# Gate-column strip moved behind the delta-rule projections; their first unit's products woven between the turns of x

## The reference, cut to what matters

```python
h = rmsnorm(x, g_mix)
proj = jnp.einsum('btd,de->bte', h, w_in)
gq, gk, gv, gr, glr, cqkv, dz, da, db = jnp.split(proj, _split_points(IN_SIZES), axis=-1)
...
gate_pre = jnp.einsum('btr,rk->btk', glr, gla_w_gate2) + gla_b_gate
...
xc = jnp.concatenate([conv_buf.astype(cqkv.dtype), cqkv], axis=1)
conv = jax.nn.silu(sum(xc[:, j:j + T] * gdn_conv_w[j] for j in range(CONV_W)))
```

## Time and profile before

| | |
|---|---|
| median of 3 runs | 1779.99 us (1779.85 to 1781.88) |
| the profiled execution, its own time | 1779.38 us |
| its span from first to last instruction | 1777.7 us |
| TensorE busy | 1753.1 us, 99% |
| VectorE, ScalarE, GpSimd busy | 1078.1, 761.8, 173.2 us |
| weights and data read | 347.84 MB |

### The profile page before, as it was taken

One profiled execution on the slowest core, in us unless ns is written; L12 is line 12 of the kernel. 1 busy time (PEld: TensorE's weight loads), 2 busy tenths in 40 slices (PEclk: granted clock), 3 DMA queues, 4 the chain that ended last, 5 costly groups with the idle time before them and its releaser, 6 DMA issues.

```text
span 1777.7 us, 35497 instructions
## 1 busy us (share of the span) xinstructions
PE 1753.1 (99%) x14527; PEld 1676.6 (94%) x14527; DVE 1078.1 (61%) x1502; ACT 761.8 (43%) x801; POOL 173.2 (10%) x170
## 2 busy tenths in 40 slices
PE   8999999999999999999999999999999999999997
PEld 6999999988999998886799999999999999999997
DVE  6778447746676776653376666665444666655444
ACT  6554546445733433433323444443333444443444
POOL 4000001001055000000035200000000000000231
PEclk9999999999999999999999999999999999999999
DMA  8555645561566679778846788885557988874553
GB/s 274 163 173 188 189 143 174 164 208 48 176 214 197 207 270 330 257 269 316 281 131 198 198 258 251 246 234 140 179 168 222 248 248 246 244 212 129 177 181 114
DMA packets 414556, 367.26 MB, mean 207 GB/s; under 512 B 11455, under 2 KB 373950, under 8 KB 413910
## 3 DMA queue, kind: packets, MB, share of 16 engines
q1 hardware_dynamic: 386792, 340.76, 62.4%
q10 hardware_dynamic: 27678, 25.26, 4.4%
HBM read 347.84 MB, written 18.35 MB: 206 GB/s over the span
## 4 chain that ended last, share of the span: by engine, by line
PE 95%; DVE 2%; DMA 1%; ACT 1%; issue 0%; DVEq 0%; SPq 0%; ACTq 0%
PE ps L479 72%; PE ps L575 10%; PE ps L556 4%; PE ps L542 1%; PE ps L1025 1%; PE ps L1554 1%; DMA gst<-in_state_gla_dram 1%; PE ps L1565 1%; PE ps L1519 1%; DVE act_lo L2282 0%; PE ps L1496 0%; PE ps L1094 0%; DVE w_lo L458 0%; PE ps L1310 0%; DVE act_hi L2281 0%; PE ps L1151 0%
## 5 line engine op out<-in xcount | busy, mean ns | idle before, releaser
L451 ACT ACTIVATE w_hi<-raw 128x2048 fp32r<-128x2048 f32 (+1 forms) x284 | 510.4, 1797 | 893.4 <-PE ps L479 723.6
L458 DVE TENSOR_TENSOR w_lo<-raw,w_hi 128x2048 fp32r<-128x2048 f32 (+1 forms) x284 | 619.3, 2180 | 296.2 <-ACT w_hi L451 294.9
L479 PE MATMUL ps<-act_hi,w_lo 128*128 128x264 f32 x2560 | 732.3, 286 | 1.0 <-DVE cst L2310 0.5
L479 PE MATMUL ps<-act_lo,w_hi 128*128 128x264 f32 x2560 | 725.6, 283 | 0.0
L479 PE MATMUL ps<-act_hi,w_hi 128*128 128x264 f32 x2560 | 725.2, 283 | 0.0
L479 PEld LDWEIGHTS ps<-act_hi,w_lo 128*128 128x128 f32 x2560 | 482.3, 188 | 3.4 <-issue 1.6
L479 PEld LDWEIGHTS ps<-act_lo,w_hi 128*128 128x128 f32 x2560 | 482.7, 189 | 0.4
L479 PEld LDWEIGHTS ps<-act_hi,w_hi 128*128 128x128 f32 x2560 | 480.1, 188 | 0.0
L479 PE MATMUL ps<-ff_hi,w_lo 128*128 128x264 f32 x704 | 201.2, 286 | 0.0
L479 PE MATMUL ps<-ff_hi,w_hi 128*128 128x264 f32 x704 | 200.2, 284 | 0.0
L479 PE MATMUL ps<-ff_lo,w_hi 128*128 128x264 f32 x704 | 199.5, 283 | 0.0
(11 more groups left out here) (455 smaller groups left out, 1932.6 us busy)
## 6 DMA issues: line engine op xcount, KB each, us to landing
raw<-in_w_in_dram SPq DMA_DIRECT2D x56, 1024.0 KB, 7.5
raw<-in_ffn_w_gate_dram SPq DMA_DIRECT2D x44, 1024.0 KB, 5.8
raw<-in_ffn_w_up_dram SPq DMA_DIRECT2D x44, 1024.0 KB, 5.9
raw<-in_ffn_w_down_dram SPq DMA_DIRECT2D x32, 768.0 KB, 4.9
raw<-in_ffn_w_down_dram SPq DMA_DIRECT2D x32, 640.0 KB, 6.1
raw<-in_w_out_dram SPq DMA_DIRECT2D x16, 1024.0 KB, 6.3
raw<-in_xa_w_q_dram SPq DMA_DIRECT2D x16, 1024.0 KB, 7.1
raw<-in_xa_w_k_dram SPq DMA_DIRECT2D x16, 1024.0 KB, 7.4
```

Source lines behind the costliest of these rows:

```text
L451: act.activation(w_part(ph, w_hi[b]), raw_part(ph, r, half), ACT.Copy)\
L458: dve.tensor_tensor(w_part(ph, w_lo[b]), raw_part(ph, r, half), w_part(ph, w_hi[b]), ALU.subtract)\
L479: mm = pe.matmul(ps[:, acc(ph, u), 0:ph.cols], w[b][:, k, :], v[:, kk + k, 0:ph.cols], start=first and k == 0 and m == 0, stop=last and k ...
```

## The change

The strip's phase goes behind gdn in the plan: its weights are asked for after gdn's last slot, its unit is multiplied after gdn's 24, and the first gla slot waits for gdn's last split. In its place at the front, gdn's first two units are asked for as 128 columns each, one behind each half of x (`load_columns`). ScalarE splits unit 0 before tile 3 of x and unit 1 before tile 12; VectorE finishes unit 0 before tile 6 and unit 1 after the last tile. TensorE turns tiles 0 to 9 of x first, then does unit 0's products of tile k and, from k = 5, turns tile k+5 ahead of them, and from k = 10 four blocks of convolution state. The copies of the turned state go from VectorE to ScalarE. The sum of squares is put into the middle of unit 1. The first four gdn units are written out on ScalarE and VectorE, with unit 3's split behind the first convolution step on ScalarE and behind the second on VectorE.

```diff
-    runs = [("strip", 1, KT), ("gdn", 12, KT), ("gla", 8, KT), ...
+    runs = [("gdn", 12, KT), ("strip", 1, KT), ("gla", 8, KT), ...
...
-            sp.wait_ge(lo_split, 2 * s + (0 if by_half else 1))
+            sp.wait_ge(lo_split, 2 * s + (2 if ph.name in ("gdn", "strip") else 0 if by_half else 1))
...
+        def load_columns(sp, m):
+            c0 = COL_GDN + m * P
+            sp.dma_start(raw[:, 0, :, m * P:(m + 1) * P], kview(wi, 0, KT, c0, P)).then_inc(raw_landed[0][m], 16)
...  (SP)
             for m, landed in enumerate((xrows_landed, second_half_landed)):
                 sp.dma_start(xrows[:, :, m * (D // 2):(m + 1) * (D // 2)], ...
-            load(sp, PH["strip"], 0, 0)
+                load_columns(sp, m)
...
-            for j in range(2):
-                load(sp, PH["gdn"], 0, j)
+            load(sp, PH["gdn"], 0, 1)
...
+            load(sp, PH["strip"], 0, 0)
             sp.wait_ge(xrows_landed, 32 + 16)
             sp.wait_ge(ssq_ready, KT)
             sp.dma_start(w2[:, :], G2[0]).then_inc(scalars_landed, 16)
+            sp.wait_ge(lo_split, PH["strip"].u0 + LO_CREDIT)
             stream("gla")
...  (TensorE)
+            ph = PH["gdn"]
+            for k in range(10):
+                turn_rows(k)
+
+            def tile_in(k):
                 pe.wait_ge(x_taken, k + 1)
+                if k >= 5 and k + 5 < KT:
+                    turn_rows(k + 5)
+                if k == 2:
...                 (turns of grows and cwrows, wait for crows)
                 if k >= 10:
                     for t in range(4 * (k - 10), 4 * (k - 9)):
                         mm = turn_conv(t)
-            for k in range(KT):
-                strip_products(k)
-            pe.wait_ge(x_ready, KT)
-            sum_squares(1, TT)
-            pe.wait_ge(cols_ready, 2)
-            ph = PH["gdn"]
-            for u in range(4):
+            products(pe, ph, 0, 0, act_hi, act_lo, ready=tile_in)
+            pe.wait_ge(cols_ready, 3)
+            products(pe, ph, 0, 1, act_hi, act_lo, middle=lambda: sum_squares(1, TT))
+            for u in (2, 3):
                 products(pe, ph, 0, u, act_hi, act_lo)
             with pe.Fori(1, ph.loops) as i:
...
+            products(pe, PH["strip"], 0, 0, act_hi, act_lo)
...  (ScalarE)
-                if k == 10:
-                    split(PH["strip"], 0, 0)
+                if k == 3:
+                    split(PH["gdn"], 0, 0)
+                if k == 12:
+                    act.wait_ge(consts_ready, 1)
+                    split(PH["gdn"], 0, 1)
...
+            split(ph, 0, 2)
             rms(1, TT, D)
-            run("gdn", gdn_take, "gla")
+            for u in range(4):
+                if u:
+                    split(ph, u // 2, (u + 2) % 4)
+                gdn_take(ph, 0, u)
+            run("gdn", gdn_take, "strip", first=1)
+            split(PH["gla"], 0, 1)
...  (VectorE)
-                if k == 11:
-                    split(PH["strip"], 0, 0)
+                if k == 6:
+                    split(PH["gdn"], 0, 0)
...
+            split(ph, 0, 1)
+            split(ph, 0, 2)
+            dve.wait_ge(cols_ready, 3)
             dve.wait_ge(rstd_ready, 1)
...
+            for u in range(4):
+                gdn(ph, 0, u)
+                if u:
+                    split(ph, u // 2, (u + 2) % 4)
+            run("gdn", gdn, "strip", first=1)
```

More of the change, by code:

```diff
@@ L87, in plan @@
 def plan():
-    runs = [("strip", 1, KT), ("gdn", 12, KT), ("gla", 8, KT), ("r", 4, KT), ("z", 4, KT), ("w_out", 8, KT), ("x_q", 8, KT),
+    runs = [("gdn", 12, KT), ("strip", 1, KT), ("gla", 8, KT), ("r", 4, KT), ("z", 4, KT), ("w_out", 8, KT), ("x_q", 8, KT),
             ("mem_k", 8, KT), ("mem_v", 8, KT), ("x_o", 8, KT), ("gu0", HALF_K, KT), ("dn0", 16, DK_),
@@ L446, in split_hi @@
             act.wait_ge(raw_landed[r][half], landed)
-            if not (ph.name in ("gu0", "gu1") or ph.wide):
+            if not (ph.name in ("gu0", "gu1") or ph.wide or n < 2):
                 act.wait_ge(raw_landed[r][1 - half], landed)
@@ L1045, in turn_rows @@
                 turn(ps[:, W4 + k % 4, T:TT], xsrow[:, k * P:(k + 1) * P]).then_inc(x_turned, 1)
[L1047 to L1057, removed]
             def turn_conv(t):
                 return turn(ps[:, 2 + t // 12, (t % 12) * 24:(t % 12) * 24 + 24], crows[:, t * P:(t + 1) * P])
-            ph = PH["strip"]
-            for k in range(KT):
+            ph = PH["gdn"]
+            for k in range(10):
                 turn_rows(k)
-                if k == 9:
+            def tile_in(k):
+                pe.wait_ge(x_taken, k + 1)
+                if k >= 5 and k + 5 < KT:
+                    turn_rows(k + 5)
+                if k == 2:
                     pe.wait_ge(cols_ready, 1)
@@ L1806, in run_with_pieces, with run @@
                     take(ph, i, u)
-            def run(name, take, nxt, before=None):
+            def run(name, take, nxt, before=None, first=0):
                 ph = PH[name]
-                with act.Fori(0, ph.loops - 1) as i:
+                with act.Fori(first, ph.loops - 1) as i:
                     for u in range(4):
@@ L1822, in run @@
                         split(ph, i, u + 2)
+                    elif nxt == "strip":
+                        split(PH["strip" if u == 2 else "gla"], 0, 0)
                     elif nxt is not None:
@@ L1843, in _ @@
                 act.activation(xsq[:, k % 4, :], x[:, k, :], ACT.Square).then_inc(sq_ready, 1)
-            split(PH["gdn"], 0, 0)
-            act.wait_ge(consts_ready, 1)
-            split(PH["gdn"], 0, 1)
-            rms(1, TT, D)
-            run("gdn", gdn_take, "gla")
+            act.wait_ge(cols_turned, 2)
+            for m in range(2):
+                ins = act.activation(cst[:, 12 * m:12 * m + 12, :].rearrange("p t (j b) -> p t b j", j=3),
+                                     ps[:, 2 + m, 0:288].rearrange("p (t b j) -> p t b j", t=12, j=3), ACT.Copy)
+            ins.then_inc(cols_ready, 1)
+            ph = PH["gdn"]
+            split(ph, 0, 2)
+            rms(1, TT, D)
+            for u in range(4):
[4 more added lines that the diff above has]
+            split(PH["gla"], 0, 1)
             c1 = consts[:, 1:2]
@@ L2260, in split, with run @@
                 split_lo(dve, ph, i, u)
-            def run(name, take, nxt):
+            def run(name, take, nxt, first=0):
                 ph = PH[name]
-                with dve.Fori(0, ph.loops - 1) as i:
+                with dve.Fori(first, ph.loops - 1) as i:
                     for u in range(4):
```

21 lines of the change are left out of this document (8 added, 13 removed).

## The result

The changed kernel takes 1784.95 us (median of 20 runs, 1782.59 to 1790.40), the kernel before 1779.68 us (20 runs, 1776.96 to 1782.06). The ratio is 1.0033 with a 95% interval of 1.0026 to 1.0041: slower by 0.33%; the medians differ by 5.3 us. That is inside the forecast range and at the upper end of its likeliest part; the likeliest case had given a loss of 2.4 us by the profile's own clock. By the prediction's line of 0.2% it is "slower", to which it had given 0.43 against 0.54 for "same". The profiled execution took 1782.78 us with a span of 1781.1, only 3.4 above the profiled one of before.

A forecast was written before the change was run, and what follows sets the result against it. TensorE, in flight 99% of the span, was taken as the bound, with 25 units behind the last turn. E + 2.7 + 14.55 + 23 x 5.81 + 0.3 ends gla's first unit at 181.3, forecasting 1782.3 us, range 1780.0 to 1792.0.

The forecast's parts named there:

- likeliest case: Clock rises in or right behind tiles 0 to 4: 1780.5 to 1785 us, chance 0.62.
- First product: Start of unit 0 on TensorE: first product at 17.45 us, after turns 7 to 9 wait for ScalarE's split.
- The woven stretch: Turns among unit 0's products: tiles 0 to 4 4.0 us; at the higher clock tiles 5 to 9 0.74 each.
- E: End of the last convolution state turn, 25.15 before: 30.1 us at the higher clock, 37.8 at the lower.
- Behind E: After the last state turn: unit 1 starts 2.7 us later, and a new 2.3 us wait stands before unit 3.
- The clock in unit 1: TensorE's clock after its rise: high from 21.45 us on in the forecast's main count, units at 5.81 us.
- a rise that is lost again: TensorE's clock at the start rises, then falls: 1785 to 1790 us, within the mixed cases given 0.13.
- Seam to gla: Passage from gdn to gla: first gla slot asked for later, 0.3 us lost, 0 to 1.5.
- Sum: Gla's first unit ends at 181.3 us, 2.4 later than 178.87.
- The rule against the change: Transposes do not count as PE busy, so woven turns could hold the clock down to unit 0's end: 1792 us.
- the first rival: Clock stays low through unit 0: last state turn 7.7 us later, time about 1791.8 us, chance 0.18.
- Why the change cannot gain: Products cannot start before 17.45 us, so most of unit 0 adds to the turning; faster got 0.03.

The follow-up runs named there:

- split3_first: Changed kernel with unit 3's weight halves made ahead of ScalarE's first take and VectorE's second convolution step, units 4 and 5 a step earlier: 1782.11 us, ratio 1.0022.
- changed_again: The changed kernel unaltered, with a second profiled execution and more timed runs: 1785.65 us, ratio 1.0039.
- filled_and_ordered: Changed kernel with 18 extra unread products in the wait before unit 1 and unit 3's halves ahead of the second convolution step: 1780.18 us, ratio 1.0004.
- split1_early: Changed kernel with VectorE's half of unit 1's split put ahead of its wait for the last turn: 1787.38 us, ratio 1.0046.
- fill_wait: Changed kernel with 18 additional products, which nobody reads, in the wait before unit 1: 1786.44 us, ratio 1.0037.
- before_plus_wait: Kernel before the change, with one more weight half on VectorE ahead of gdn's first unit: 1782.63 us, ratio 1.0016.
- sum_in_wait: Changed kernel with the sum of squares in the wait before unit 1 instead of the middle of unit 1: 1781.53 us, ratio 1.0017.
- turns_first: Changed kernel without the weaving, all turns done ahead of unit 0 and all else kept: 1782.04 us, ratio 1.002.

## Why the prediction held, and where it was too small

- **The bound** was read rightly: 25 units follow the last turn, and the loss is made before them and between them.
- **First product**, 17.45 forecast: 16.80 in the first profile, 17.16 to 17.47 in the six others that weave. The first profile is the odd one: x's first half was there at 6.50, in all twelve others, before among them, between 6.84 and 7.16. The turns waited 1.47 for ScalarE, as the split at tile 3 had it. Tiles 0 to 4 took 3.84 us, 4.0 forecast. The clock was high right behind them, as in the likeliest case. That the rise of the profile before was early (3.2 us behind the first product) had no row behind it then; the thirteen profiles bear it out, with 3.0 to 7.0 us.
- **The woven stretch** was mis-sized. I gave a woven tile 0.74 us at the higher clock; the profile has 0.95. The two turns of x in a tile take 0.31 there and xsrow's turn 0.16, so 0.47 for what I had put at 0.29 from the earlier trace rows. Halving the rows of the same instructions, 0.82 a tile, would have given 0.41 and been close: the turns of x are halved, xsrow's is not. Six turns of yT in 0.58 are another sequence, and a tile of x isn't three of them. Tiles 5 to 9 took 5.0 us (20.64 to 25.62) instead of 3.7, 0.27 of it because the clock rose within the first; the state turns took 5.3 instead of 4.95. Less the early start, E came at 30.97 instead of 30.1, and in an execution with x at its usual time it is half a microsecond later still.
- **Behind E**, 2.7 forecast, 2.8 measured; the wait of 2.3 before unit 3 came as worked out, through the chain named. Split3_first shows what it costs: 2.8 us of the median, 2.1 with each kernel against its own "before", 3.5 against changed_again beside it.
- **The clock in unit 1** is the step that failed. I had a high clock once reached stay high in the likeliest case, and "a rise that is lost again" only as part of the 0.13 between. It was lost in both profiles of this kernel. In the first, unit 1's 24 products before the sum took 4.42 us instead of 2.9, so 1.5 us; in the second that and 3.7 more, over four places. The prediction gave 1785 to 1790 to a rise that is lost again, and the median lies at the lower end of that.
- **Seam to gla**, 0.3 forecast: 0.42 of waiting for VectorE, behind a DMA that lands late (7.87 us in the chain). Its unit then takes 6.07 instead of 5.81, another 0.26: 0.1 is its first product, which behind a wait holds the next for 0.23 instead of 0.12, and the rest the end of a last product, which shows only ahead of a wait.
- **Sum**: 0.85 + 0.1 + 1.5 + 0.1 + 0.26 = 2.8, and with the 2.4 forecast 5.2, against 5.4 measured at the end of gla's first unit. That the medians give 5.3 too is partly luck: the usual execution starts half a microsecond later and loses between one and three stretches of clock.
- **The rule against the change** was weighed and half right. The clock rose between 20.9 and 24.4 in the woven profiles, amid the woven turns in six of the seven and on the last products ahead of them in filled_and_ordered. From the rule of the Trainium skill ("TensorE: Matmul & The Clock Gate", Part 4: PE-mode transpose, that transposes do not count as PE busy as matmuls do) one could have expected them to hold it down, and they did not: the first rival's 1792 did not come. But the granted clock did not hold: in three profiles it fell while TensorE was still at the woven steps or on their last products (31.04, 31.13 and about 31.5). There the trace agrees with the rule, though it doesn't show that the turns are the cause. I should have given it a price in the likeliest case, a fallen stretch of some 1.5 us, rather than a place among the mixed cases.
- **Why the change cannot gain** was right. Unit 0 of the changed kernel ends at about 31.5, the strip of before at 32.5, so the weaving hides one microsecond, of which half is x's early landing in that execution. Then it pays 2.2 at unit 1 and 2.3 at unit 3. Without the weaving and with both orders mended the change is neutral (0.9996). With the weaving, unit 3's order mended and the wait filled it can't be told from "before" either (1.0004 [0.9995, 1.0013]), but beside it its median is 1.5 us higher.

What stays open is the state part: 91.6 to 95.7 us from one execution to another, with the clock column below 1 somewhere between 444 and 468 when it is long. It is untouched by the change. Its lengths follow the low clock in it: 91.58 to 91.74 in the five profiles that have none, 93.17 to 93.69 in the five with about 3.4 us of it, 94.52 and 94.58 with 6.8, 95.73 with 10.2. What is open is why one execution has it and another not. The medians of split1_early and fill_wait are above the changed kernel's, and both profiles had the longest state parts (94.58 and 95.73). With 5 and 6 runs I can't tell whether a shifted start makes that likelier or whether it is chance. Nor was it settled whether the wait or the weaving pulls the clock down in unit 1 of the first profile. Fill_wait kept the clock up and before_plus_wait lost some on average, which speaks for the wait. Filled_and_ordered, changed_again and sum_in_wait lost it before any wait, split3_first within 1 us of one and split1_early behind 0.76 us, which speaks for the weaving.

## What to carry to other kernels

Weaving transposes between matmuls hides only the waits that TensorE had: where the turns already ran back to back, a tile turned among products still takes its own time (0.47 us at the higher clock here) plus 0.11 for the first product behind it, and a low-clock stretch came with it in six of seven profiles. When a unit is moved to the front, list for each engine queue what now stands ahead of the next two operands; here the order of one split was worth 2.3 us of wait and the place of one DMA issue up to 2.9, more than the move could win. And a wait of over 2 us is to be priced with the half-speed stretch that followed it in four of seven profiles here, about 1.5 us, not only with itself. Last, a wait that is gone from one profile may be gone because a low clock made TensorE late: see where the engine would have been.

## What the runs showed of the hardware

- Two executions of the same kernel differed by 5.1 us within the first 190 us, 3.7 of it by the clock (ends of gla's first unit 184.25 and 189.33). Over 20 executions of it the time went from 1782.6 to 1790.4 us as the mean granted clock went from 0.997 to 0.992.
- In twelve of the thirteen profiles (all but turns_first) the clock was low again somewhere between its first rise and 470 us, for some 3 us at the least and 10 at the most, with products at half their rate. It first rose 3.0 to 7.0 us behind the first product.
- A float32 turn of 128x128 took 0.31 us at the lower clock and 0.155 at the higher, the 8-row turn 0.20 and 0.16, though it has 8 columns instead of 128; a tile of turns goes from 0.82 to 0.47. Four state turns between products took 0.35 us at the higher clock and 0.55 at the lower.
- The first product behind float32 turns started its successor 0.23 us later instead of 0.12 at the higher clock, and 0.39 instead of 0.22 at the lower.
